# A two-layer encoder step on one core: z tiles in pair order with the first pair prepared in stage z, and the output projection's first two tiles started inside the last pair

## The reference, cut to what matters

```python
x = layer_norm(ALPHA * x + 0.5 * swiglu(x, ffn1_w_in[i], ffn1_w_out[i]), ...)
z = x @ w_in[i]                                # 1024 -> 256 (u) + 2560 (zr)
u, zr = z[..., :256], z[..., 256:]
zs = zr + (z_prev - zr) * mu_shift             # z_prev: the token before
r, k, v, lw, la, lg = split(zs)                # 768, 768, 768, 64, 64, 128
# decay, a, kk (normalised by head), k; then the state recurrence of 12 heads,
# layer norm by head, bonus (sum of r*k*r_k) * v, times the gate sigmoid(lg) @ g2
mix = concat([pool_mixer(u), rwkv_out]) @ w_out[i]          # 1024 -> 1024
x = layer_norm(ALPHA * x + mix, ...)
# then a second feed-forward part and a per-layer input embedding, each added to x
```

## Time and profile before

| what | us |
|---|---|
| median of 3 runs (2867.34 to 2868.11) | 2867.54 |
| the profiled execution's own time | 2867.53 |
| its span, first to last instruction | 2865.5 |
| TensorE busy in the span | 2675.4 (93%) |
| VectorE busy | 1203.6 (42%) |
| ScalarE busy | 668.9 (23%) |
| GpSimd busy | 1579.9 (55%) |
| mean granted TensorE clock, share of full speed | 0.973 |

### The profile page before, as it was taken

One profiled execution on the slowest core, in us unless ns is written; L12 is line 12 of the kernel. 1 busy time (PEld: TensorE's weight loads), 2 busy tenths in 40 slices (PEclk: granted clock), 3 DMA queues, 4 the chain that ended last, 5 costly groups with the idle time before them and its releaser, 6 DMA issues. The chain is left out here.

```text
span 2865.5 us, 65195 instructions
## 1 busy us (share of the span) xinstructions
PE 2675.4 (93%) x27580; PEld 2581.1 (90%) x27580; DVE 1203.6 (42%) x1641; ACT 668.9 (23%) x1267; POOL 1579.9 (55%) x1244
## 2 busy tenths in 40 slices
PE   8999998888887999999999999988888879999997
PEld 8999998867776999999999999987777779999997
DVE  2111139755554761111574111597455547511114
ACT  3221012244432231100241000123444213211002
POOL 5666665613323666666766666656233146666665
PEclk9999999889998999999999999998899989999998
DMA  4222322100000222332322222221000012223322
GB/s 153 88 86 83 89 88 68 58 2 4 4 19 24 87 84 86 96 89 82 105 82 88 88 85 87 86 62 42 3 3 4 19 46 81 88 88 94 89 81 77
DMA packets 61801, 192.54 MB, mean 67 GB/s; under 512 B 11456, under 2 KB 11712, under 8 KB 61632
## 3 DMA queue, kind: packets, MB, share of 16 engines
q1 hardware_dynamic: 57600, 185.95, 21.3%
q10 hardware_dynamic: 4032, 4.08, 0.4%
HBM read 186.88 MB, written 3.12 MB: 66 GB/s over the span
## 5 line engine op out<-in xcount | busy, mean ns | idle before, releaser
L527 PE MATMUL ps<-xh,w_hi 128*128 128x272 f32 x3648 | 766.9, 292 | 65.6 <-POOL w_lo L499 24.1
L497 POOL TENSOR_SCALAR w_hi<-w_raw 128x1024 fp32r<-128x1024 f32 (+2 forms) x364 | 380.6, 1046 | 709.6 <-PE ps L527 700.8
L527 PE MATMUL ps<-xl,w_hi 128*128 128x272 f32 x3648 | 766.9, 292 | 0.0
L527 PE MATMUL ps<-xh,w_lo 128*128 128x272 f32 x3648 | 762.0, 290 | 0.0
L527 PEld LDWEIGHTS ps<-xh,w_hi 128*128 128x128 f32 x3648 | 580.7, 191 | 71.4 <-issue 60.3
L501 POOL TENSOR_TENSOR w_lo<-w_raw,w_hi 128x640 fp32r<-128x640 f32 (+2 forms) x364 | 615.6, 1691 | 0.0
L527 PEld LDWEIGHTS ps<-xh,w_lo 128*128 128x128 f32 x3648 | 583.9, 192 | 0.0
L527 PEld LDWEIGHTS ps<-xl,w_hi 128*128 128x128 f32 x3648 | 583.7, 192 | 0.0
L499 POOL TENSOR_TENSOR w_lo<-w_raw,w_hi 128x384 fp32r<-128x384 f32 x364 | 406.8, 1118 | 30.4
L1321 DVE TENSOR_TENSOR hf<-sg,ps 128x544 f32<-128x544 f32 x76 | 54.8, 721 | 611.1 <-PE ps L527 611.1
L527 PE MATMUL ps<-hh,w_hi 128*128 128x272 f32 x1472 | 305.2, 289 | 0.0
(11 more groups left out here) (286 smaller groups left out, 3848.0 us busy)
## 6 DMA issues: line engine op xcount, KB each, us to landing
w_raw<-in_w1i SPq DMA_DIRECT2D x88, 512.0 KB, 3.6
w_raw<-in_w2i SPq DMA_DIRECT2D x88, 512.0 KB, 3.6
w_raw<-in_wz SPq DMA_DIRECT2D x44, 512.0 KB, 3.6
w_raw<-in_w1o SPq DMA_DIRECT2D x32, 448.0 KB, 3.3
w_raw<-in_w2o SPq DMA_DIRECT2D x32, 448.0 KB, 3.3
w_raw<-in_wgp SPq DMA_DIRECT2D x32, 320.0 KB, 2.8
w_raw<-in_w1o SPq DMA_DIRECT2D x16, 512.0 KB, 3.5
w_raw<-in_wo SPq DMA_DIRECT2D x16, 512.0 KB, 3.6
```

Source lines behind the costliest of these rows:

```text
L497: pool.tensor_scalar(w_hi[k][:, 0:nk, :], w_raw[k][:, 0:nk, :], 1.0, 0.0, ALU.mult, ALU.add).then_inc(w_hi_done, 1)
L527: mm = pe.matmul(ps[:, 2 * pair + h, 0:n], w[:, j, :], x[:, kx, h * HT:h * HT + n], start=(start and q == 0), stop=(stop and q == 2))
```

## The change

- The tiles of stage z come in the order r0, k0, v0, r1, k1, v1 and so on (`Z_ROWS`; the weights are laid out in this order). `zb` and `zd` move to other memory, and `zd` has two buffers.
- The difference to the token before is no longer formed. ACT computes `zd` = `mu` times the previous token (`z_blend`), with the copy of the last rows and the patch of the sample's first token; DVE's last operation of a tile multiplies z by 1 - `mu` and adds `zd`.
- `pooling` of the first u tile comes after the first tile of step 2, that of the second after step 3; `gained` comes after steps 4 and 5 (four each); ACT's `scaled` after the pieces of steps 5 and 6, so the eviction of the mixer stands ahead of it.
- The first pair's pieces run one step earlier, the first pair's Newton iteration (five operations, as four) moves from POOL to DVE, and `prepare_2` of the first pair runs in steps 8 and 9 of stage z (POOL's part after the split of step 9). PE's first transposes of the heads wait for the banks of the last tiles.
- The copies `lora_st` and `g2_st` on DVE go; PE reads the full tensors.
- For the last pair: POOL splits the first two slots of stage wo before the last half, and then makes `xh` and `xl` of the first five pairs' rows (`early_rows`) once the last block product is done. PE issues the gate matmul at k = 5 of the last half and 14 k tiles of stage wo early (`early_out`): tile 0's k tiles 0 to 3, one behind each of the last chunks, 4 to 6 behind the mean matmul, and tile 1's 0 to 6 behind the variance matmul. The three POOL products of this pair's norm are done by DVE. Then only one row is copied and split, `last_row` does the eighth k tile of both output tiles and marks both slots as used, and `dense` goes on from step 1.

The diff, cut to its core:

```diff
...
+Z_ROWS = [r + p for p in range(NPAIR) for r in (0, NPAIR, 2 * NPAIR)]
...
-        zb = [sb(f"zb{i}", [P, T + 8]) for i in range(2)]
-        zd = sb("zd", [P, T])
...
+        top[0] = zr_addr + 4 * 3 * 64 * 4
+        zb = [sb(f"zb{i}", [P, T + 8]) for i in range(2)]
+        zd = [sb(f"zd{i}", [P, T]) for i in range(2)]
...
+        def head_norm(p):
+
+            return (gn, prs) if p < NPAIR - 1 else (aa, kkb)
...
-        IN_A = {0: (0,), 1: (1,), 2: (2,), 3: (3, 4), 4: (5,), 9: (10,)}
+        IN_A = {1: (1,), 2: (2,), 3: (3, 4), 4: (5,), 9: (10,)}
         IN_B = {0: (0,), 1: (1,), 3: (6,), 9: (8, 9)}
         POOL_B = 3
         Z_POOLED, Z_LAST = 5, 5
-        Z_PIECES = {5: (0,), 6: (1,), 7: (2, 3), 8: (4, 5), 9: (10,)}
-        PIECES_2 = range(10)
+        Z_PIECES = {5: (1,), 6: (2, 3), 7: (4, 5), 8: (10,)}
+        Z_PIECES_2 = {8: (6, 8, 9), 9: (0, 1)}
...
-                if k == 5:
+                if k == 5 and p > 0:
...
+                if p == NPAIR - 1:
+                    return
...
+            def early_rows(l):
+
+                pool.wait_ge(t_mm[1], (l + 1) * NPAIR * NSTEP)
+                for p in range(NPAIR - 1):
+                    pool.wait_ge(po_ready, l * NPAIR + p + 1)
+                    pool.tensor_scalar(xh[:, p + 2, 0:T], zs[:, p, :], 1.0, 0.0, ALU.mult, ALU.add).then_inc(xh_ready, 1)
+                    pool.wait_ge(xh_ready, l * 32 + p + 11)
+                    pool.tensor_tensor(xl[:, p + 2, 0:T], zs[:, p, :], xh[:, p + 2, 0:T].bitcast(F32), ALU.subtract).then_inc(xl_ready, 1)
+
             def half_a(l, p, left, right, nxt):
+                if not left:
+                    split(l, "wo", 0, (8, 8))
+                    early_rows(l)
...
-                        for k in PIECES_2:
-                            prepare_2(l, 0, k, True)
...
+                    with pool.Fori(int(name == "wo"), last) as m:
+                        split(l, name, m, ks)
                     for m in range(last, bodies):
-                        split(m)
+                        split(l, name, m, ks)
 
                         for q in Z_PIECES.get(m - 1, ()):
                             prepare_1(l, 0, q, True)
+                        for q in Z_PIECES_2.get(m - 1, ()):
+                            prepare_2(l, 0, q, True)
...
-                    pe.wait_ge(staged, n + 1)
-                    two(5, lora_st[0:64, :], lora[0:64, :]).then_inc(wa_mm, 1)
+                    if p == 0:
+                        pe.wait_ge(lora_act, l * 2 + 2)
+                        pe.wait_ge(layer_loaded, l * 32 + 32)
+                    two(5, lora_all[0:64, p * P:p * P + P], lora[0:64, :]).then_inc(wa_mm, 1)
...
+                if p == NPAIR - 1 and k in (1, 3):
+                    early_out(l, *((4, 7) if k == 1 else (7, 14)))
+                if k == 5 and p < NPAIR - 1:
 
                     if inner:
                         pe.wait_ge(t_out[0], n * NSTEP + 2 * NSTEP)
-                    pe.wait_ge(g_staged, n + 1)
-                    two(3, g2_st[:, :], lgate).then_inc(pg_mm, 1)
+                    two(3, g2_all[:, p * P:p * P + P], lgate).then_inc(pg_mm, 1)
+
+            def early_out(l, start, stop):
+
+                n = l * SLOTS + SLOT0["wo"]
+                for q in range(start, stop):
+                    tile, c = q // (KT - 1), q % (KT - 1)
+                    if c == 0:
+                        pe.wait_ge(tile_out[tile], out_count(l, "wo", 0) - 1)
+                        pe.wait_ge(w_first, n + tile + 1)
+                        if tile == 1:
+
+                            pe.wait_ge(g_ready, (l + 1) * NPAIR)
+                    if c == WF:
+                        pe.wait_ge(w_split, n + tile + 3)
+                    pe.wait_ge(xl_ready, l * 32 + c + 9)
+                    three(tile, tile, c, xh, xl, c, c == 0, False)
+
+            def last_row(l):
+                for tile in range(2):
+                    pe.wait_ge(xl_ready, l * 32 + 16)
+                    three(tile, tile, KT - 1, xh, xl, KT - 1, False, True).then_inc(slot_used, 1)
...
+                            used += [(tile_out[k], out_count(l, "z", NZ // 2 - 1)) for k in range(2)]
...
+                    if not left and k == 5:
+                        two(3, g2_all[:, (p - 1) * P:p * P], lgate).then_inc(pg_mm, 1)
+                    if not left and k > 5:
+                        early_out(l, k - 6, k - 5)
...
+                last_row(l)
+                dense(l, "wo", xh, xl, xl_ready, l * 32 + 8, start=1)
...
+            def z_blend(l, m, k, j, order):
+                i = l * NSH + order
+                z = zb[k]
+
+                act.wait_ge(zc_ready, i + 1)
+                act.activation(zd[k][:, :], z[:, 0:T], ACT.Copy, scale=col(l, j + COL["mu"])).then_inc(zd_ready, 1)
+                act.activation(flat(last_z[:, j:j + 1, :]), z[:, TP:T + 1:TS], ACT.Copy).then_inc(last_ready, 1)
+                act.wait_ge(zd_ready, i * 2 + 1)
+                act.activation(zd[k][:, TP:TP + 1], shift_in[:, l, j:j + 1], ACT.Copy, scale=col(l, j + COL["mu"])).then_inc(zd_ready, 1)
+
+            def z_tile(l, m, k):
+                z_weights(l, m, k)
+                z_shift(l, m, k)
+                z_blend(l, m, k, Z_ROWS[2 * m - 4 + k], 2 * m + k - 2)
...
+                    for k in range(4 * (m - 5), 4 * (m - 4)) if m < 7 else ():
+                        scaled(l * 3, k, t_ready, l * 24 + k + 1)
...
-                with act.Fori(0, NPAIR) as p:
-
-                    act.wait_ge(po_ready, (l + 1) * NPAIR)
-                    act.activation(row(xh, p + 2), row(zs, p), ACT.Copy).then_inc(xh_ready, 1)
+
+                act.wait_ge(po_ready, (l + 1) * NPAIR)
+                act.activation(xh[:, NPAIR + 1, 0:T], zs[:, NPAIR - 1, :], ACT.Copy).then_inc(xh_ready, 1)
...
-                dve.tensor_tensor(zd[:, :], z[:, 0:T], z[:, 1:T + 1], ALU.subtract).then_inc(zd_ready, 1)
-
-                dve.tensor_copy(last_z[:, bass.ds(j, 1), :].rearrange("p a s -> p (a s)"), z[:, TP:T + 1:TS]).then_inc(last_ready, 1)
-                dve.wait_ge(zd_ready, i * 2 + 1)
-
-                dve.tensor_tensor(zd[:, TP:TP + 1], flat(shift_in[:, bass.ds(l, 1), bass.ds(j, 1)]), z[:, TP + 1:TP + 2],
-                                  ALU.subtract).then_inc(zd_ready, 1)
                 dve.wait_ge(zd_ready, i * 2 + 2)
-                dve.scalar_tensor_tensor(dst, zd[:, :], col(l, j + COL["mu"]), z[:, 1:T + 1], ALU.mult, ALU.add).then_inc(zs_ready, 1)
+                dve.scalar_tensor_tensor(dst, z[:, 1:T + 1], col(l, j + COL["one_mu"]), zd[k][:, :], ALU.mult, ALU.add).then_inc(zs_ready, 1)
...
+                    if p == 0:
+                        dve.wait_ge(rn_ready, n + 1)
+                        dve.tensor_tensor(nt[:, :], nv[:, :], rn[:, :], ALU.mult).then_inc(kk_newton, 1)
+                        dve.wait_ge(kk_newton, n * 4 + 1)
+                        dve.scalar_tensor_tensor(nt[:, :], nt[:, :], -0.5, rn[:, :], ALU.mult, ALU.mult).then_inc(kk_newton, 2)
+                        dve.wait_ge(kk_newton, n * 4 + 3)
+                        dve.scalar_tensor_tensor(rn[:, :], nt[:, :], 1.5, rn[:, :], ALU.add, ALU.mult).then_inc(kk_newton, 1)
+                        dve.wait_ge(kk_newton, n * 4 + 4)
+                        dve.tensor_tensor(kkb[:, :], rn[:, :], kkb[:, :], ALU.mult).then_inc(kkb_ready, 1)
...
+                if p < NPAIR - 1:
+                    return
+                if k == 4:
+                    dve.wait_ge(hn_newton, n * 3 + 3)
+                    dve.tensor_tensor(pd[:, :], pd[:, :], head_norm(p)[1][:, :], ALU.mult).then_inc(pt_ready, 1)
+                if k == 6:
+                    dve.wait_ge(pi_ready, n + 1)
+                    dve.tensor_tensor(psq[:, :], psq[:, :], row(zs, p + 6), ALU.add).then_inc(pb_ready, 1)
+                    dve.wait_ge(pb_ready, n + 1)
+                    dve.wait_ge(g_ready, n + 1)
+                    dve.tensor_tensor(row(zs, p), psq[:, :], head_norm(p)[0][:, :], ALU.mult).then_inc(po_ready, 1)
...
+                tile(2, 0)
+                pooling(l, 0)
+                tile(2, 1)
                 for k in range(2):
-                    pooling(l, k)
-                    shifted(l, 2, k, k, 2 + k, zs[:, k, :])
-                for m in range(3, Z_LAST):
-                    for k in range(2):
-                        shifted(l, m, k, 2 * m + k - 4, 2 * m + k - 2, zs[:, 2 * m + k - 4, :])
-                    for k in range(4 * (m - 3), 4 * (m - 2)):
-                        gained(l * 3, k)
+                    tile(3, k)
+                pooling(l, 1)
+                for k in range(2):
+                    tile(4, k)
+                for m in range(KT // 2):
+                    gained(l * 3, m)
...
+                        tile(m, k)
                     if m == Z_LAST:
+                        for k in range(KT // 2, KT):
+                            gained(l * 3, k)
...
-                dve.wait_ge(zs_ready, l * NSH + NSH + 2)
```

(20 more changed lines are left out.)

87 lines of the change are left out of this document (41 added, 46 removed).

## The result

The changed kernel took 2829.86 us (median of 4 executions, 2825.28 to 2837.64) beside 2867.82 of the kernel before on the same chip: ratio 0.9869, 95% interval 0.9845 to 0.9893. It is faster by 38 us where 61 were forecast. The execution with the profile took 2825.28 us; its span is 2823.4, 42.1 less than the span before.

What follows compares the result with a forecast made beforehand. PE bounds the kernel except where a side engine's queue holds it, each hold also costing clock. Gains of 38.5 (z), 7.0 (heads) and 15.2 (tail), 60.7 us off 2867.53, give 2807 us; range 2785 to 2833, eight in ten.

Steps and rivals of the forecast that it cites:

- The floor of z: Stage z, fifth slot's end to last: 108.8 us without any stall, plus 1.1 for a product moved in.
- What comes back in z: Stage z: stalls remaining after the change, 3.0 us of PE waits and 1.5 of lost clock, 4.5 a layer.
- it is worked off within four slots and PE evicts late by none: Stage z: the first pair's Newton step on VectorE fits some 1.5 us of slack in each slot.
- Rival (c): Stage z: the round trip over ACT keeps VectorE late, only half of z's gain comes, 2826 us; chance 0.15.
- Heads: Change from z to the heads: ACT evicts the transposes sooner, `products` start earlier; gain 3.5 us a layer.
- Tail: End of the heads, last pair's chunks to output tile 2 of stage wo: gain 7.6 us a layer.
- The half clock for the chunks: Last pair's chunks: the page's busy but slow stretch was taken to persist; four k tiles there take 4.2 us.
- rival (a): Last pair's chunks: full clock comes back early, 2 x 4.5 us more gain, 2798 us; chance 0.17.
- the ends: End of the heads: gain 2.4 us a layer if everything stays slow, 12.1 at full clock from the start.
- the chain to the last row: End of the heads: ACT and VectorE operations with nine handoffs, from the variance to the last row, 8.2 us.

Runs made afterwards that it cites:

- a_again: The changed kernel run again with nothing altered: 2831.26 us, ratio 0.9863 to the kernel before.
- j_order: f_fill and g_warm together, plus pool products moved between two z tiles, Newton step and scaled rows re-ordered, first pair's transposes evicted earlier: 2789.33 us, ratio 0.9712.
- b_lora: Changed kernel with ACT's tanh and sigmoid done earlier and four transfer issues put behind z tile (2,0): 2829.67 us, ratio 0.9860.
- c_newton: Changed kernel with VectorE evicting z tile (8,0) before the first pair's Newton step instead of after it: 2833.26 us, ratio 0.9861.
- f_fill: b_lora plus VectorE's stage z re-ordered: single operations fill the waits for ACT, poolings dealt out over five tiles: 2829.77 us, ratio 0.9869.
- h_dveblend: Changed kernel with the multiplication of z by mu moved back from ACT to VectorE: 2837.96 us, ratio 0.9891.
- g_warm: Changed kernel plus six products that nothing reads in each of the last pair's four sparse steps before the chunks: 2815.04 us, ratio 0.9812.

## Why the prediction was right or wrong

- **Direction and range: right.** 2829.9 lies in 2785 to 2833, near its slow end. The point, 2807, was 23 us too fast, and in part it is luck that the miss was no larger: in the profiled execution z gained 20.7 us less than forecast, while the heads and the tail gained 5.7 more. They would have gained less than forecast if layer 0's tail had lost the full clock, as it did in a_again, for 8 us.
- **The floor of z: right.** "Without any stall the stretch would be 108.8", plus 1.1, is 109.9; j_order shows 110.2 and 110.3.
- **What comes back in z: the step that failed.** The term was 4.5 us a layer, 3.0 of waits and 1.5 of clock; it measured 125.2 - 110.2 = 15.0 and 124.3 - 110.3 = 14.0 (11.9 and 12.8 in a_again). Of the first, 10.1 is more empty time and 4.8 the same 839 matmuls at a lower clock (114.53 against 109.69 busy). Two things went wrong. I laid out VectorE's queue alone: its idle time in a tile, "with handoffs 1.4 us", was near (1.2 in the trace), and a queued tile took no more than the 4.5 us of the forecast (3.4 from 543.07, 4.3 from 464.50), but ACT's queue ahead of the first of these tiles, 5.7 us of issues, table loads and activations, was not in it. And "it is worked off within four slots and PE evicts late by none", of the Newton step, did not hold: the slack of 1.5 us a slot was already used. b_lora and c_newton show that neither stall is an error of one place: each comes back at the next tile. f_fill and j_order show what it was: idle times of 1.2 us and blocks of 3.5 to 8 us on a VectorE that has hardly any slack at these places.
- **Rival (c)** is what happened by size: half of z's gain, 2826. I gave it 0.15. By mechanism it is half of it: the round trip over ACT takes VectorE's slack, but the waits came where a block of other work stood ahead of an eviction, and f_fill, which fills the round trips, took off 1 to 2 us a layer until j_order had moved the blocks too. Its argument against, 4.5 us a tile under 6.08 a slot, took a mean over a stage whose fixed blocks fall on certain tiles. h_dveblend adds that a tile's wait for ACT is worth about what the work was: moving it off VectorE bought 1.7 us a layer as long as nothing filled the wait.
- **Heads:** 3.5 forecast, 5.5 and 3.7 measured, and 1.6 and 5.5 in a_again, so one profile does not fix this term; ACT evicted at 5.5 us behind the last slot, not 6.3. The Trainium skill's drain of 1.38 us behind a table load (ScalarE: Activation LUTs, What ACT_TABLE_LOAD costs) is not in this trace either: the load at 453.36 lasts 1.28 and the activation starts at 454.65.
- **Tail:** the forecast, 34 us from chunk to tile 2, lies between two cases, 27.8 and 36. The half clock for the chunks was right for most, rival (a) for the rest. The size of each was near (29.5 and 39.2 forecast for the ends); the cause of the short one was put wrongly. Two small slips lie in the working: tile 2 of the kernel before started at 926.25, not 926.5, and the chain to the last row adds up to 8.0 us, not 8.2; it measured 7.7 (887.06 to 894.74). No full clock came back among the chunks: from 2260 to 2280 us PE is 18.2 us busy, dense matmuls among small ones, and stays at 0.50. In the short tail the clock had not fallen before or in the chunks. What decides is the sparse steps before the chunks, as long as the chunks themselves are filled: g_warm shows it by filling the steps. TensorE: Matmul & The Clock Gate in the Trainium skill (Part 1) has activity release the throttle. Here the trace agrees only in part: 18.2 busy us of 20 did not release it, and it came back behind the chunks, at 1.00 from 2284 to 2290 us, under dense matmuls without a gap.

## What to carry to other kernels

When work leaves an engine that paces others, lay out the queue of every engine that it now waits for, with the blocks at their places and at the speed they have beside their neighbours, and not a mean per tile against a mean slot. A wait that vanishes at one tile and returns at the next means a queue that is full there: deal the long blocks out between tiles, fill the handoffs, and then take out the waits that are left together, for here the last of these steps brought nearly all of the gain. And work used as filler should start before the stretch in which the clock falls, for at half clock it costs twice what it would cost behind it (1.6 us a k tile against 0.76).

## What the runs showed of the hardware

The same seven VectorE operations took 3.5 us with GpSimd idle and 7.6 beside its splits (b_lora). The same program ran the tail of layer 0 at full clock in one execution and at half in another, 8 us apart; that this makes up most of its spread of 2824 to 2838 us is likely but not shown, since only two of its executions were traced. The last pair's sparse steps, in which no gap of PE is longer than 0.93 us, left the clock up in layer 0 of one execution and stood just ahead of its fall in another. And 24 products a layer that nothing reads, some 2.7 us of work, made the kernel 16 us faster.
